# A two-layer streaming encoder step with its loops written out, x taken tile by tile and weight loads reordered

## What is computed

```python
hn = rmsnorm(x, norm_mix)
parts = split_columns(hn @ w_in)          # 23 units of 128 columns
# A: gated DeltaNet (conv width 4 on q/k/v, chunk-wise delta rule)
# B: sliding-window attention with sinks   C: latent attention   D: short gated conv
x = x + jnp.concatenate([o_a, o_b, o_c, o_d], axis=-1) @ w_out
x = x + squared_relu(rmsnorm(x, norm_mlp) @ mlp_w1) @ mlp_w2      # width 4096
x = x + (p[l] @ ple_w_proj) * sigmoid(rmsnorm(x, norm_ple) @ ple_w_gate)
```

## Time and profile before

| | |
|---|---|
| three runs, median (lowest to highest) | 1723.1 us (1720.34 to 1723.92) |
| the profiled execution: time, span | 1719.4 us, 1717.6 us |
| TensorE matmuls: busy, share, count | 1590.0 us, 93%, 14582 |
| VectorE / GpSimd / ScalarE busy | 925.4 / 643.4 / 497.5 us |
| mean granted TensorE clock | 0.97 of full speed |
| moved by DMA | 122.46 MB, mean 71 GB/s |

### The profile page before, as it was taken

One profiled execution on the slowest core, in us unless ns is written; L12 is line 12 of the kernel. 1 busy time (PEld: TensorE's weight loads), 2 busy tenths in 40 slices (PEclk: granted clock), 3 DMA queues, 4 the chain that ended last, 5 costly groups with the idle time before them and its releaser, 6 DMA issues.

```text
span 1717.6 us, 36187 instructions
## 1 busy us (share of the span) xinstructions
PE 1590.0 (93%) x14582; PEld 1505.2 (88%) x14582; DVE 925.4 (54%) x1474; ACT 497.5 (29%) x838; POOL 643.4 (37%) x313
## 2 busy tenths in 40 slices
PE   4889998799999999999887999987999999999996
PEld 4879777589999999999877897766999999999995
DVE  4765477546536171664466655764473543617553
ACT  6422233432111111133254213333321111111332
POOL 2335121145444344454432441210643444444652
PEclk9999999889999999999988999998999999999998
DMA  5111011032222222222221110111322222222221
GB/s 173 62 51 39 27 39 52 4 88 86 88 88 95 87 85 85 85 86 79 88 63 53 48 39 26 42 36 18 100 86 93 91 87 86 85 85 85 87 85 65
DMA packets 43804, 122.46 MB, mean 71 GB/s; under 512 B 10960, under 2 KB 13776, under 8 KB 43536
## 3 DMA queue, kind: packets, MB, share of 16 engines
q1 hardware_dynamic: 43520, 118.74, 22.4%
q10 hardware_dynamic: 144, 1.78, 0.3%
HBM read 116.75 MB, written 3.76 MB: 70 GB/s over the span
## 4 chain that ended last, share of the span: by engine, by line
PE 55%; issue 31%; POOL 10%; ACT 1%; DVE 1%; DMA 1%; POOLq 0%; SPq 0%; DVEq 0%; ACTq 0%
PE psum_p L1315 55%; POOL w_rest L547 7%; POOL factor_t L577 2%; ACT hidden_a L651 1%; DMA constants<-consts 1%; POOL x_squares_summed L559 0%; POOL inverse_t L572 0%; POOL inverse_t L570 0%; ACT w_high L632 0%; DMA x<-x_t 0%; DVE y L1288 0%; DVE ple_out L1273 0%; DVE x L1266 0%; PE psum_t L1300 0%; ACT x_squared L657 0%
## 5 line engine op out<-in xcount | busy, mean ns | idle before, releaser
L547 POOL TENSOR_TENSOR w_rest<-raw,w_high 128x1024 fp32r<-128x1024 f32 x210 | 516.2, 2458 | 926.5 <-ACT w_high L632 926.5
L1315 PE MATMUL psum_p<-hidden_a,w_high 128*128 128x272 f32 x3520 | 602.2, 293 | 39.3 <-DVE hidden_a L902 33.4
L1315 PEld LDWEIGHTS psum_p<-hidden_a,w_high 128*128 128x128 f32 x3520 | 508.2, 192 | 44.3 <-DVE hidden_a L902 34.2
L632 ACT ACTIVATE w_high<-raw 128x1024 fp32r<-128x1024 f32 x210 | 222.4, 1059 | 826.2 <-PE psum_p L1315 781.3
L1315 PE MATMUL psum_p<-hidden_b,w_high 128*128 128x272 f32 x2560 | 429.8, 290 | 8.1 <-POOL w_rest L547 4.7
L1315 PEld LDWEIGHTS psum_p<-hidden_b,w_high 128*128 128x128 f32 x2560 | 365.8, 190 | 10.0 <-issue 10.0
L1315 PE MATMUL psum_p<-hidden_a,w_rest 128*128 128x272 f32 x1760 | 368.5, 291 | 0.0
L1315 PEld LDWEIGHTS psum_p<-hidden_a,w_rest 128*128 128x128 f32 x1760 | 279.7, 191 | 0.0
L1315 PE MATMUL psum_p<-hidden_b,w_rest 128*128 128x272 f32 x1280 | 265.9, 289 | 0.0
L1160 DVE TENSOR_TENSOR x<-psum_p,x 128x544 f32<-128x544 f32 x80 | 58.0, 724 | 292.9 <-PE psum_p L1315 292.9
L1315 PEld LDWEIGHTS psum_p<-hidden_b,w_rest 128*128 128x128 f32 x1280 | 201.2, 189 | 0.0
(11 more groups left out here) (252 smaller groups left out, 1545.4 us busy)
## 6 DMA issues: line engine op xcount, KB each, us to landing
raw<-w_units SPq DMA_DIRECT2D x210, 512.0 KB, 3.5
x<-x_t SPq DMA_DIRECT2D x8, 272.0 KB, 4.4
y_t<-y SPq DMA_DIRECT2D x8, 272.0 KB, 2.1
constants<-consts ACTq DMA_DIRECT2D x1, 1737.5 KB, 9.1
ple_in<-p_t SPq DMA_DIRECT2D x2, 544.0 KB, 7.3
w_kv<-w_kv SPq DMA_DIRECT2D x2, 256.0 KB, 4.6
ckv_p<-mla_c SPq DMA_DIRECT2D x2, 256.0 KB, 2.1
mla_c<-ckv_cache SPq DMA_DIRECT2D x2, 128.0 KB, 4.1
```

The lines of the kernel that those rows point to most:

```text
L547: mark(pool.tensor_tensor(wlo[:, u % SPLIT, :], raw[:, u % RAW, :], whi[:, u % SPLIT, :].bitcast(F32), ALU.subtract), lo_done)
L632: mark(act.activation(whi[:, u % SPLIT, :], raw[:, u % RAW, :], ACT.Copy), hi_done)
L1315: ins = pe.matmul(pp[:, 2 * b + h, 0:HALF], w[:, s, cols(k)], rhs[:, k, part, h * HALF:(h + 1) * HALF], start=(n == 0 and z == 0), stop=(n ...
```

## The change

1. All hardware loops (layers, MLP groups, on all engines) are written out; wait values are constants, and `wait_apart` no longer waits on `first`. The rings of weight slots and PSUM slots run on from layer to layer (`ring`, `slot(l, o)`).
2. At the start each tile of x has a semaphore of its own. SyncE issues parameters, unit 0, x tiles 0 and 1, unit 1, the other six tiles. ScalarE and VectorE do `norm_high`, square, `norm_split` and sum for each tile as it lands; `constants` is issued behind the sixth `norm_high`.
3. `hidden_a` and `hidden_b` swap roles in layer two (two buffers `hidden_0`, `hidden_1`; the scratch tiles exist once per layer). So `norm_high`/`norm_split` of layer two's tiles 0 to 6 run inside layer one's PLE block, and `high` of layer two's units 0 and 1 behind the last gate units.
4. TensorE takes units 0 and 1 together (`first_units`): at the start interleaved with the tiles, in layer two all tiles but the last of both, then the last; `sum_x` comes behind both.
5. SyncE loads units U_OUT+2 and U_OUT+3 ahead of the 14 stores and U_OUT+4 ahead of p. The split of p moves from ahead of the MLP into its first group.

```diff
         def wait_apart(eng, *targets):
-            targets = [(sem, eng.to_reg(value)) for sem, value in targets]
-            eng.wait_ge(first.sem, 16)
             for sem, value in targets:
                 eng.wait_ge(sem, value)
...
-            with sp.Fori(0, DEPTH) as l:
+            load_parameters(0)
+            for l in range(DEPTH):
-                for u in range(RAW):
-                    load_unit(l, u)
+                load_unit(l, 0)
+                for m in range(KT if l == 0 else 0):
+                    sp.dma_start(x[:, m, :], x_t[:, m, :]).then_inc(x_in[m].sem, 16)
+                    if m == 1:
+                        load_unit(l, 1)
+                if l:
+                    load_unit(l, 1)
...
-                for u in range(RAW, U_OUT + RAW):
+                load_unit(l, 2)
+                if l:
+                    sp.wait_ge(*proj.at(l, 0))
+                sp.dma_start(conv_in[l][:, :, SEQ + 3:SEQ + 6], ...
+                for u in range(3, U_OUT + 2 * RAW):
                     load_unit(l, u)
...
+                load_unit(l, U_OUT + 2 * RAW)
                 sp.wait_ge(*mixed_a.at(l, 2))
                 sp.dma_start(pin[:], one(p_t, l).rearrange("a p k n -> p (a k) n")).then_inc(ple_in.sem, 16)
...
+            act.wait_ge(*gains_in.at(0, 16))
+            high(0, 0)
             for m in range(KT - 1):
+                norm_high(0, 0, m)
+                if m == 2:
+                    high(0, 1)
+                if m == 5:
+                    act.dma_start(cst[:], consts).then_inc(first.sem, 16)
                 square_x(0, 0, m)
...
                     if u < UNITS:
                         high(l, u)
+                    elif l + 1 < DEPTH:
+                        if u == UNITS:
+                            act.wait_ge(*gains_in.at(l + 1, 16))
+                        high(l + 1, u - UNITS)
                     act.wait_ge(*gate_in.at(l, m + 1))
...
                         square_x(l, 3, m)
+                        if l + 1 < DEPTH:
+                            norm_high(l + 1, 0, m)
...
                 def add_gated(m):
                     gate = [xr, sqt][m % 2][:]
+                    if m and l + 1 < DEPTH:
+                        norm_split(l + 1, 0, m - 1)
                     dve.wait_ge(*gated.at(l, m + 1))
...
+            def first_units(l):
+                if l:
+                    order = [(0, k) for k in range(KT - 1)] + [(1, k) for k in range(KT - 1)] + [(0, KT - 1), (1, KT - 1)]
+                else:
+                    order = [(u, k) for i in range(KT + 2) for u, k in ((0, i), (1, i - 2)) if 0 <= k < KT]
+                for i, (u, k) in enumerate(order):
+                    b, s = slot(l, u), ring(l, u, SPLIT)
+                    if k == 0:
+                        pe.wait_ge(*lo_done.at(l, u + 1))
+                        pe.wait_ge(*freed.at(l, u - 1))
+                    if u == 0:
+                        pe.wait_ge(*normed.at(l, k + 1))
```

More of the change, by code:

```diff
@@ L102, in __init__ @@
         self.made = 0
-        self.loop = 0
     def at(self, layer, n):
@@ L108, in now @@
     def now(self, layer):
-        return self.sem, layer * self.per + (self.made + self.head) + self.loop
+        return self.sem, self.made + self.head
 def tasks():
@@ L313, in signal @@
             return every[-1]
-        landed = [signal(f"landed_{s}", 16 * len(range(s, UNITS, RAW))) for s in range(RAW)]
+        landed = [signal(f"landed_{s}", 0) for s in range(RAW)]
         gains_in = signal("gains_in", 16)
@@ L321, in build @@
         stored = signal("stored", 16 * 14, 1)
-        x_in = signal("x_in", 0)
+        x_in = [signal(f"x_in_{m}", 0) for m in range(KT)]
         first = signal("first", 0)
@@ L586, in mid_unit @@
                             factor(l, a[1] + 1, b)
-            with pool.Fori(0, DEPTH) as l:
+            for l in range(DEPTH):
                 wait_apart(pool, normed.at(l, 0))
@@ L603, in _ @@
                     add_square(l, 1, m)
-                with pool.Fori(0, GROUPS - 1) as g:
-                    for i in range(2 * KT):
-                        rest(l, U_MLP + SPLIT + i, g)
-                lo_done.made += (GROUPS - 2) * 2 * KT
+                for i in range(2 * KT * (GROUPS - 1)):
+                    rest(l, U_MLP + SPLIT + i)
                 for i in range(2 * KT):
@@ L767, in mid_unit @@
                         step(l, *a)
+            act.wait_ge(*gains_in.at(0, 16))
+            high(0, 0)
             for m in range(KT - 1):
[L770 to L777 removed]
+                norm_high(0, 0, m)
[3 more added lines that the diff above has]
+                    act.dma_start(cst[:], consts).then_inc(first.sem, 16)
+                square_x(0, 0, m)
+            for l in range(DEPTH):
+                norm_high(l, 0, KT - 1)
                 square_x(l, 0, KT - 1)
@@ L843, in _ @@
                         inv_rms(l, 1)
-                with act.Fori(1, GROUPS - 1) as g:
-                    for i in range(2 * KT):
-                        high(l, U_MLP + SPLIT + i, g)
-                hi_done.made += (GROUPS - 3) * 2 * KT
+                for i in range(2 * KT * (GROUPS - 2)):
+                    high(l, U_MLP + SPLIT + i + 2 * KT)
                 for i in range(2 * KT):
@@ L1162, in mlp_group, with add_out, split_ple @@
-            def mlp_group(l, g, g0, last):
+                    split_to(l, lambda z: hb[l][:, 4:6, z, i * P:i * P + rows], src, mixed)
+            def add_out(l, o, m):
+                dve.wait_ge(*proj.at(l, o + 1))
+                link(dve, dve.tensor_tensor(two(x[:, m, :]), psum_of(l, o), two(x[:, m, :]), ALU.add), freed, l)
+            def split_ple(l):
+                dve.wait_ge(*ple_in.at(l, 16))
+                step(dve.tensor_copy(ph[:, :, 0, :], pin[:]), l)
+                mark(dve.tensor_tensor(ph[:, :, 1, :], pin[:], f(ph[:, :, 0, :]), ALU.subtract), ple_sp)
@@ L1507, in mid_unit @@
                         step(l, *a)
-            with pe.Fori(0, DEPTH) as l:
-                for u in range(N_PRE):
-                    for item, *a in HOOKS[2 * u - 2] if u else []:
+            for l in range(DEPTH):
+                first_units(l)
+                sum_x(l, 0)
+                assert U_CKV > 1 and U_V0 > 1
+                for u in range(2, N_PRE):
+                    for item, *a in HOOKS[2 * u - 2]:
                         if item == "rope":
@@ L1516, in _ @@
                             pe.wait_ge(*c_r.at(l, 1))
-                    product(l, u, u, ha, range(KT), between=lambda: mid_unit(l, 2 * u),
-                            ready=(lambda k: pe.wait_ge(*normed.at(l, k + 1))) if u == 0 else None)
-                    if u == 0:
-                        sum_x(l, 0)
+                    product(l, u, u, ha[l], range(KT), between=lambda: mid_unit(l, 2 * u))
                     mid_unit(l, 2 * u + 1)
@@ L1606, in build @@
         wrong = {s.sem.name: (s.made, s.per) for s in every
-                 if s.made and s.made != s.per}
+                 if s.made and s.made != DEPTH * s.per}
         assert not wrong, wrong
```

292 lines of the change are left out of this document (141 added, 151 removed).

## The result

| | before | changed |
|---|---|---|
| median of 4 runs (lowest to highest) | 1721.7 us (1718.6 to 1723.9) | 1682.8 us (1682.1 to 1684.3) |
| ratio, with its 95% interval | | 0.9776 (0.9758 to 0.9795) |
| span of the profiled execution | 1717.6 us | 1680.3 us |
| TensorE idle, worked out as span less its busy time | 127.6 us | 100.5 us |
| lost to the slow clock | 34.5 us | 23.0 us |

A forecast was written before the change was run, and what follows sets the result against it. TensorE, busy for 93%, was taken as the bound, with gains only at its pauses. Terms -5.5 - 3.4 - 6.2 - 1.3 = -16.4 gave 1703.0 us against the profiled execution, 1706.7 against the median; forecast 1705, range 1695 to 1714.

The forecast's parts named there:

- What bounds the kernel: Whole kernel: TensorE is busy for 93% of the span, so the change can win only where TensorE stands, at the edges.
- Start, -5.5: Program start: first matmul at 8 to 10 us instead of 21.7, unit 3 6.2 us earlier; -5.5 us, bounds -8 and -2.
- Seam, -3.4: Between the layers: TensorE's pause of 9.38 us becomes about 2.5; -3.4 us after clock loss, bounds -7 and 0.
- Output projection, -6.2: Output projection: loading U_OUT+2 earlier removes pauses of 2.50 and 2.24 us plus 1.5 of clock; bounds -4.7 and -6.5.
- Loops, -1.3: Written-out loops: no gain at the MLP, attention between none and 3 us per layer; -1.3 us taken in all.
- Clock: Half-speed stretches behind pauses: 1.7 us lost at the start, 2.5 at the seam, 1.5 regained at the output projection.
- more is kept: Rival, start, seam, output and loops: clock holds in the new pauses and VectorE is on time; 1696 us, chance 0.20.
- Slower: Rival, written-out MLP loops: fetching about 20 more code packets stops TensorE; 1727 us at 1.2 us each, chance 0.04.
- The sign of being wrong: MLP and attention: holes in the MLP, or an attention phase of another length than before by over 3 us.

## Why the prediction was wrong

- **What bounds the kernel**: right. TensorE's pauses and the clock behind them hold the whole difference; the inside of the MLP has neither hole nor change.
- **Start, -5.5**: right, and a little small; 7.2 us in the stages. The pauses came where forecast and a little shorter (2.35 and 2.90 us for some 3 and 4). One term was off: `norm_split` was priced at 1.31 us, stretched; beside no `rest` it takes 0.77 us, and the last tile's was over at 20.5, not 22.5. The clock took 1.4 us more than before, 1.7 were set.
- **Seam, -3.4**: 2.7 us beyond the loops. The pause is 1.51 us (2.5 forecast), the next two 2.34 and 1.46 (3 and 4); against that, the `norm_split` between the copies cost 1.9 us beside the kernel with its loops written out, not 0.8. The 9.7 us that the stage gained in all include 6.9 of the loop.
- **Output projection, -6.2**: 7.9 us alone, the right mechanism. (What the prediction calls the second output unit is U_OUT+2, here the third.) The trace of before could not show the 12.2 that the medians give it behind the loops, but the question "what is late next" was only asked for the moved load, not for what would arrive there sooner.
- **Loops, -1.3**: the step that failed; measured 14.6 us. The prediction chose the MLP's rows as "nearest" because TensorE shows no hole there, and wrote that "the branch of the layer loop is part of the seam", without a price. But at the seam it is ScalarE that TensorE waits for, and the timeline of before has its stall: `ACT_TABLE_LOAD` with [2.38 <-issue] at 860.14. The prediction read the rule of the Trainium skill as one for every turn of a loop and set it aside because the MLP loop shows no hole. But the rule is for a target outside the fetched window, and the records agree with that: 0.2 to 0.3 us behind the branches of the short MLP loops, 2.7 and 2.8 us behind those of the layer loop. The upper bound of 3 us per layer counted attention alone, where the runs give 1.2.
- **Clock**: counted as a price of new pauses (+1.7, +2.5, -1.5: 2.7 us worse); in fact 11.5 us better, 14 us of the miss. The old pauses had longer slow stretches behind them, one of 20.5 us with 14.95 of matmuls in it. The two windows of 6 us in the earlier trace rows were too small a sample to see them. The 11.5 cut across the other terms: by one profile each, 4.5 of it came with the loops and 6.8 with the loads behind them; with the loads moved alone the one profile lost 3.9 more instead, so this division is loose.
- **Rivals**: "more is kept", 1696, was on the right side, but it too left the loops at 3 us and the old clock out. "Slower" by code fetch did not show: MLP windows of straight code are as dense as before. The sign of being wrong, an attention phase of another length by over 3 us, depends on where the phase ends. The phase proper gave 1.7 us for both layers; counted from the same matmul to the first output unit's product it is 2.4 us shorter in layer one and 4.7 in layer two, so there the sign was seen. With two output units counted, the end gave 6.6 per layer.

## What to carry to other kernels

Price a loop's branch at each engine that someone waits for, not at the busiest one: look behind the branch for an "issue" gap and a table load that straight code would not have. Add up, from the granted clock, what the slow stretches cost now, before removing pauses: here each us of idle TensorE removed came with 0.4 us of clock (11.5 for 27.1), between two profiles; a single step can stray from that (the loads alone: 5.6 us less idle, 3.9 more lost). Two edits that shorten the same chain can be worth more together than apart, when the first alone only runs into what the second moves; here the pause that shows it grew by 1.3 us in both layers together.

## What was new about the hardware

- A taken branch of the layer loop left ScalarE idle for 2.38 us (2.68 from the branch to the next instruction; 2.78 on VectorE, 4.13 on SyncE), and a table load of 1.28 us followed on ScalarE. The taken branches of the MLP loops on ScalarE and VectorE, with 49 and 89 recorded instructions from turn to turn, were followed by the next instruction within 0.3 us, as was GpSimd's layer branch (329), and writing the MLP loops out changed nothing (1.0002, 0.9987 to 1.0018).
- In these rows the same VectorE instruction took 0.29 us where it started 0.11 us ahead of a GpSimd instruction and 2.44 us where it started 0.05 us behind it. VectorE is held in both kernels; which of its instructions is held moved TensorE's pause by 1.3 us. The Trainium skill, "SBUF — State Buffer", section "SBUF: two separate sides", says that the one that starts first holds their shared port for its whole instruction; the two rows agree.
- The same pause of 2.0 us behind the same matmuls was followed by 3.4 us at half clock in one profile and by none in another. What decides it is open.
- Open is how the layer loop's 12 us divide between the stall and the arithmetic on wait values. Of idle TensorE the seam's pause gave 3.3 us and attention 1.3 per layer; the rest is clock and what follows from both.
